# Mixer input stage: a fourth z unit ahead of the first group, ScalarE instead of VectorE reads the turned step sizes, sums over tokens placed ahead of the taps

## What is computed

```python
def mamba2_mixer(u, w_in, conv_w, conv_b, dt_bias, a_log, ...):
    z, xbc, dt_raw = split(u @ w_in, [2048, 2048 + 4096])
    conv = conv_b + sum(xbc_full[:, k:k + t_len] * conv_w[k] for k in range(4))
    xs, bm, cm = split(silu(conv), ...)            # per head, per group
    dt = softplus(dt_raw + dt_bias)
    a = -exp(a_log)
    y, h_last = ssd_scan(xs, dt, a, bm, cm, ssm0)  # chunks of 128 tokens
    ...
def ssd_scan(...):
    cum = cumsum(dtc * a)                          # over the tokens of a chunk
    decay = exp(where(causal, cum_t[l] - cum_t[s], -inf))
    y_intra = einsum(cb * decay, xdt)
    to_end = exp(cum_last - cum)
    ...
```

## Time and profile before

| | |
|---|---|
| median of 3 runs | 1200.87 us (1199.36 to 1201.12) |
| the profiled execution | 1198.53 us |
| its span, first to last instruction | 1196.7 us |
| TensorE (PE) busy | 1186.5 us, 99% |
| VectorE (DVE) busy | 873.0 us, 73% |
| ScalarE (ACT) busy | 696.4 us, 58% |
| GpSimd (POOL) busy | 247.1 us, 21% |

### The profile page before, as it was taken

How to read it: one execution, slowest core, us unless ns; L and a number is a source line. 1 busy time by engine, 2 the same in 40 slices (tenths; PEclk the granted TensorE clock), 3 DMA queues, 4 the chain that set the end, 5 groups by cost and what they waited for, 6 DMA issues and landing times.

```text
span 1196.7 us, 26588 instructions
## 1 busy us (share of the span) xinstructions
PE 1186.5 (99%) x9797; PEld 1157.8 (97%) x9797; DVE 873.0 (73%) x1398; ACT 696.4 (58%) x1132; POOL 247.1 (21%) x351
## 2 busy tenths in 40 slices
PE   9999999999999999999999999999999999999998
PEld 9999999998989899999999999999998899999998
DVE  7667646999999868666745988787468767667448
ACT  6454435777686657555546765555368764544345
POOL 1000002423222202122344333232026310000001
PEclk9999999999999999999999999999999999999999
DMA  8765554755445375866886677656742256555552
GB/s 290 255 202 185 176 178 142 256 181 182 158 160 179 117 219 185 327 216 248 279 299 230 211 269 284 220 172 235 245 163 74 90 167 211 177 181 185 176 178 87
DMA packets 62144, 239.08 MB, mean 200 GB/s; under 512 B 7288, under 2 KB 8480, under 8 KB 57696
## 3 DMA queue, kind: packets, MB, share of 16 engines
q1 hardware_dynamic: 55728, 197.01, 49.0%
q0 software_dynamic: 6064, 40.66, 9.3%
q10 hardware_dynamic: 288, 0.54, 0.1%
HBM read 226.87 MB, written 13.39 MB: 201 GB/s over the span
## 4 chain that ended last, share of the span: by engine, by line
PE 91%; DVE 5%; ACT 2%; issue 1%; DMA 0%; POOL 0%; SPq 0%; DVEq 0%; ACTq 0%
PE bank L479 28%; PE bank L480 28%; PE bank L481 28%; DVE wlo L1520 1%; DVE xact L1788 1%; PE bank L843 1%; DVE xl L1539 1%; PE bank L838 1%; PE bank L652 1%; PE bank L865 1%; PE bank L638 0%; PE bank L895 0%; DMA raw<-weights 0%; ACT whi L1050 0%; PE bank L622 0%
## 5 line engine op out<-in xcount | busy, mean ns | idle before, releaser
L1520 DVE TENSOR_TENSOR wlo<-raw,whi 128x1024 fp32r<-128x1024 f32 x367 | 456.6, 1247 | 237.6 <-ACT whi L1050 236.3
L479 PE MATMUL bank<-xh,whi 128*128 128x264 f32 x2008 | 576.0, 287 | 2.5 <-DVE under L1567 1.5
L480 PE MATMUL bank<-xl,whi 128*128 128x264 f32 x2008 | 569.2, 283 | 0.0
L481 PE MATMUL bank<-xh,wlo 128*128 128x264 f32 x2008 | 568.8, 283 | 0.0
L1050 ACT ACTIVATE whi<-raw 128x1024 fp32r<-128x1024 f32 x367 | 385.4, 1054 | 243.7 <-PE bank L481 231.7
L479 PEld LDWEIGHTS bank<-xh,whi 128*128 128x128 f32 x2008 | 378.2, 188 | 5.9 <-DVE wlo L1520 2.3
L480 PEld LDWEIGHTS bank<-xl,whi 128*128 128x128 f32 x2008 | 378.4, 188 | 0.9
L481 PEld LDWEIGHTS bank<-xh,wlo 128*128 128x128 f32 x2008 | 376.6, 188 | 0.0
L479 PE MATMUL bank<-hh,whi 128*128 (+1 forms) x896 | 255.5, 285 | 0.3 <-ACT gu L1403 0.3
L481 PE MATMUL bank<-hh,wlo 128*128 (+1 forms) x896 | 255.1, 285 | 0.0
L480 PE MATMUL bank<-hl,whi 128*128 (+1 forms) x896 | 254.4, 284 | 0.0
(11 more groups left out here) (331 smaller groups left out, 1024.2 us busy)
## 6 DMA issues: line engine op xcount, KB each, us to landing
raw<-weights SPq DMA_DIRECT2D x367, 512.0 KB, 3.5
under<-ssm POOLq DMA_DIRECT2D x8, 1024.0 KB, 7.3
xact<-ssm POOLq DMA_DIRECT2D x8, 1024.0 KB, 7.8
out_ssm_s<-xact POOLq DMA_DIRECT2D x8, 1024.0 KB, 5.6
xact<-dtx_rows POOLq DMA_DIRECT2D x5, 1024.0 KB, 11.0
zs<-dtx_rows POOLq DMA_DIRECT2D x2, 1024.0 KB, 14.2
x<-xT SPq DMA_DIRECT2D x4, 264.0 KB, 5.6
xact<-stat_rows POOLq DMA_DIRECT2D x2, 528.0 KB, 6.5
```

The source lines that it names most:

```text
L479: pe.matmul(out, whi[:, w, c], rh, start=start, stop=False)
L480: pe.matmul(out, whi[:, w, c], rl, start=False, stop=False)
L481: return pe.matmul(out, wlo[:, w, c], rh, start=False, stop=stop)
L1520: dve.tensor_tensor(wlo[:, s, :], raw[:, s, :], whi[:, s, :].bitcast(F32), ALU.subtract).then_inc(lo_ready, 1)
```

## The change

The order of units becomes dt, z, z, z, z, conv x4 (units 5 to 8), z (9), conv x4 (10 to 13), z (14); from unit 9 on it is as it was. `PRE_AT` becomes 8. TensorE turns in slot 8 and sums in slot 10 as before. ScalarE, in slot 9, copies `dtT` and `da4` out of bank 4 and signals TensorE with a new semaphore `pre_t`; VectorE keeps only `dgl`, now in slot 9. The series for the step sizes is cut 3, 3, 1 over slots 2 to 4 instead of 4, 3 over slots 2 and 3. ScalarE's `cum4` comes in slot 11, ahead of its tap, and `select(0)` with the exponentials in slot 13. VectorE's `pre_sums` comes in slot 11 and `pre_diff` in slot 12, both ahead of the taps of the slot, and `pre_decode` stays in slot 13. ScalarE's doubled high half (units 5 and 6 rounded in a row) is in slot 5 instead of 4 (there units 4 and 5), and the gathers with it. The counts of `pre_d` are one lower. The weights are packed by `SIN`, so the loads follow.

```diff
-Z_FIRST = [0, 1, 2]
-Z_AFTER = {0: [3, 4], 1: [5], 2: [6], 3: [7], 4: [8], 5: [9], 6: [10], 7: [11, 12, 13, 14, 15]}
+Z_FIRST = [0, 1, 2, 3]
+Z_AFTER = {0: [4], 1: [5], 2: [6], 3: [7], 4: [8], 5: [9], 6: [10], 7: [11, 12, 13, 14, 15]}
-PRE_AT = 7
+PRE_AT = 8
# TensorE
-                pe.wait_ge(pre_d, 1)
+                pe.wait_ge(pre_t, 1)
                 for c in range(2):
...
                 mm.then_inc(pre_p, 1)
-                pe.wait_ge(pre_d, 2)
+                pe.wait_ge(pre_d, 1)
                 pe.matmul(bank[7][:, 0:256], ones[32:64, :], dgl[32:64], start=True, stop=True)
...
-                if s_ == PRE_AT + 3:
+                if s_ == PRE_AT + 2:
                     pre_sums()
# ScalarE
-                if 1 < s_ < len(SIN) and s_ != 5:
+                if 1 < s_ < len(SIN) and s_ != 6:
                     ahead("sin", 0, s_)
-                if s_ == 4:
-                    ahead("sin", 0, 5)
+                if s_ == 5:
+                    ahead("sin", 0, 6)
                     gather_sizes()
+                if s_ == PRE_AT + 3:
+                    act.wait_ge(pre_p, 2)
+                    act.activation(cum4, bank[2][:, 0:256], ACT.Copy).then_inc(pre_a, 1)
+                if s_ == PRE_AT + 1:
+                    act.wait_ge(pre_p, 1)
+                    for c in range(2):
+                        act.activation(dtT[c], bank[4][:, 64 * c + 32:64 * c + 64], ACT.Copy)
+                        ins = act.activation(da4[c].rearrange("p (k h) -> p k h", k=4), bank[4][:, 64 * c:64 * c + 32].unsqueeze(1).to_broadcast([P, 4, HEADS]), ACT.Copy)
+                    ins.then_inc(pre_t, 1)
                 if kind == "conv":
                     tap_last(s_, i)
...
-                if s_ == 4:
+                if s_ == 5:
                     gather_steps()
...
-                if s_ == PRE_AT + 3:
-                    act.wait_ge(pre_p, 2)
-                    act.activation(cum4, bank[2][:, 0:256], ACT.Copy).then_inc(pre_a, 1)
                 if s_ == PRE_AT + 5:
-                    act.wait_ge(pre_d, 4)
+                    act.wait_ge(pre_d, 3)
# VectorE
             def pre_tokens():
-                dve.wait_ge(pre_p, 1)
-                for c in range(2):
-                    dve.tensor_copy(dtT[c], bank[4][:, 64 * c + 32:64 * c + 64])
-                    ins = dve.tensor_copy(da4[c].rearrange("p (k h) -> p k h", k=4), bank[4][:, 64 * c:64 * c + 32].unsqueeze(1).to_broadcast([P, 4, HEADS]))
-                ins.then_inc(pre_d, 1)
+                dve.wait_ge(dt_a_step, 5)
...
+                if s_ == PRE_AT + 3:
+                    pre_sums()
+                if s_ == PRE_AT + 4:
+                    pre_diff(0)
+                    pre_diff(1)
                 if last == "conv":
                     conv_taps(li)
...
                 if s_ == 2:
-                    dt_series((15, 13, 11, 9))
+                    dt_series((15, 13, 11))
                 if s_ == 3:
-                    dt_series((7, 5, 3))
+                    dt_series((9, 7, 5))
+                if s_ == 4:
+                    dt_series((3,))
                     dt_end()
                 if s_ == PRE_AT + 1:
                     pre_tokens()
-                if s_ == PRE_AT + 3:
-                    pre_sums()
-                if s_ == PRE_AT + 4:
-                    pre_diff(0)
-                    pre_diff(1)
-                if s_ == PRE_AT + 6:
+                if s_ == PRE_AT + 5:
                     pre_decode()
```

More of the change, by code:

```diff
@@ L268, in trunk_kernel @@
         pre_d = sem("pre_d")
+        pre_t = sem("pre_t")
         pre_a = sem("pre_a")
@@ L1251, in select @@
                 if k == 1:
-                    act.wait_ge(pre_d, 5)
+                    act.wait_ge(pre_d, 4)
                 if k >= 2:
```

## The result

The changed kernel takes 1203.55 us, the median of nine runs (1201.56 to 1205.10), and the kernel before 1199.36 beside it, also of nine (1198.13 to 1201.12). The ratio is 1.0033, 95% interval 1.0025 to 1.0042: about 4.0 us slower. The profiled execution after took 1203.79 us with a span of 1202.0; the one before had 1198.53 and 1196.7. The forecast was 1203.5, on a base of 1200.87 that has turned out 1.5 us too high: direction and place were right, the amount (2.6) was not the whole of it.

What follows compares the result with a forecast made beforehand. TensorE, busy 1186.5 of 1196.7 us, was taken to bound the kernel. The terms -1.44 + 1.63 + 2.27 + 0.17 gave +2.6 us, on 1200.87 a forecast of 1203.5, range 1200.9 to 1205.2.

Steps and rivals of the forecast that it cites:

- What bounds the kernel: Whole kernel: TensorE, busy 1186.5 of 1196.7 us; a change wins or loses only where TensorE stands waiting.
- The hole at unit 9: TensorE's wait for VectorE's take of unit 7: that take comes earlier, 1.44 us gained, 0.2 of the hole left.
- The last sums: Ahead of unit 11: TensorE waits for VectorE's diagonal products, now in slot 9; the 1.44 is spent and 0.19 more, +1.63.
- The copies on ScalarE: Turned step sizes in slot 9: ScalarE needs 0.5 to 1.4 us, taken as 0.7; either bound costs nothing.
- The selection: Head of the first chunk: sums queued behind the take of unit 11 delay ScalarE's first selection; unit 15 2.45 late, term +2.27.
- The first decay: Behind the selection: table load, exponentials, then VectorE's decay product; VectorE 2.63 late at the low half of slot 13, term +0.17.
- The sum: All terms together: -1.44 + 1.63 + 2.27 + 0.17 = +2.6 us.
- rival (c): Behind a larger TensorE hole the granted clock falls to 1.2 GHz; 2.9 us per unit of 24 matmuls, 1206.4; chance 0.03.
- The base: Time of the kernel before that the forecast was added to: 1200.87 us, the median of the runs shown.

Runs made afterwards that it cites:

- e1_dgl8: The changed kernel with VectorE's diagonal products in slot 8 instead of slot 9; 1200.21 us against 1198.49 for the kernel before.
- e6_copies: The kernel before with only the four copies of the turned step sizes moved to ScalarE; 1198.33 us against 1198.58, ratio 0.9998.
- e4_fill: The changed kernel with 11 useless matmuls ahead of the last sums and 16 ahead of the selection; 1201.39 us against 1198.49 for the kernel before.
- e7_late: The kernel before with only sums, differences and selection one slot later, sums and differences ahead of the taps; 1200.90 us against 1198.58.
- e10_after: The changed kernel run and profiled once more without an edit; 1203.99 us against 1198.66 for the kernel before, ratio 1.0043.
- e2_sums10: The changed kernel with sums, differences and first selection one slot earlier, sums and differences behind the taps; 1201.13 us against 1198.49 for the kernel before.

## Why the prediction was right, and where it was short

- **What bounds the kernel.** Right. In the two profiles 4.89 of the 5.3 us in span arise between the common matmul and unit 17; 0.25 lie ahead of it, in the first microseconds of the program, and 0.2 behind unit 17.
- **The hole at unit 9, -1.44.** Measured -1.44, with 0.24 us left of it (forecast 0.2). The take of unit 7, read from starts of rows, held to the hundredth.
- **The last sums, +1.63.** Measured +1.52 (from -1.44 to +0.08). TensorE stood 1.34 us at L928 for VectorE's diagonal products. e1_dgl8 shows the cause: one slot earlier, and 1.29 us come back.
- **The copies on ScalarE, nothing.** Right: four in 0.6 us, between the bounds of 0.5 and 1.4, and off the path. e6_copies alone is worth nothing.
- **The selection, +2.27.** Measured +2.27 (from +0.08 to +2.35) in e4_fill, where the clock plays no part, and +2.25 (from +0.03 to +2.28) in e7_late. The chain behind it held too: on the clock of the kernel before, e4_fill's selection starts at 252.95, against 252.96 in the prediction. The reading was that VectorE would be idle for 2.6 us ahead of the sums; counted on the clock of the changed profile it is 3.92, of which 1.5 belong to a unit 11 that ran at half clock.
- **The first decay, +0.17.** e4_fill has +0.23 (from +2.35 to +2.58), with a hole of 0.4 us left at the decay product. ScalarE's table load took 1.28 us again and the decay began 3.12 us after the selection, 3.13 before. By the figure of the Trainium skill's "ScalarE: Activation LUTs" (Step-by-step: what each stage is for), about 2.7 us with the drain, the sum would have been an estimated 4.0, and the median did move by that; but the row says 1.28 with nothing idle behind it, so the missing 1.4 stood elsewhere. A right total from a wrong term would have been easy to believe here.
- **The sum.** The bare schedule costs 2.58 us by e4_fill's profile and 2.9 by its ratio (1.7 to 4.0), against 2.6 forecast.
- **The step that fell short** is rival (c). The prediction named it, asked for 0.03 of the chance with the words "the trace so far bears it out nowhere within the stage", and left it out of the sum. It took the full clock behind one hole of 1.48 us as evidence for the next holes. The runs show that the clock behind such a hole differs between executions: behind the hole of 1.3 us at L928 it fell in one of three profiles (the changed kernel yes; e10_after and e2_sums10 no), behind the hole of 1.9 to 2.0 us at the selection in four of four (the changed kernel, e10_after, e1_dgl8, e7_late), and with both filled in none. Four of four is no rate: the profiled executions of e1_dgl8 and e7_late, with a mean clock of 0.996, are the slowest and the second slowest of eleven each, and the other twenty have 0.998 to 1.000. Its price was right in kind and too high in amount: 15 or 16 matmuls at 1.2 GHz, 1.5 us, instead of a whole unit of 24, 2.9. The Trainium skill's "TensorE: Matmul & The Clock Gate" (Part 1, What's actually happening) calls the number of slow matmuls at the start of a kernel run-variable, as the chip does not time the transition from the kernel's start. The traces agree that it varies, here in the middle of a kernel: 2 falls and 1 in the stage in two executions of one kernel (+4.89 and +3.38 at unit 17).
- **What is left.** The ratio says +4.0 us (3.0 to 5.0). With no fall, one and two the profiles give +2.6, +3.4 and +4.9, and the nine runs lie 2.2 to 5.7 us above 1199.36, nearly in the order of their mean granted clock: 1201.56 at 0.999, 1203.55 and its neighbours at 0.997, 1205.10 at 0.995. That the middle runs have one or two falls in this stage is argued from this and not shown: only two executions were profiled, a late fall as in e10_after can be among them, and the mean clock also takes in the last microseconds of the program (0.62 from 1195 us on in the kernel before).

The base was a smaller slip. The forecast stood on 1200.87, the median of three runs, while 21 to 33 runs of the same kernel in the other comparisons have medians of 1198.49 to 1198.66. On 1199.36 the forecast of 2.6 gives 1202.0, which is 1.6 below the measured time. That 1203.5 met 1203.55 is luck: this error and the missing falls cancel.

## What to carry to other kernels

Work moved off a saturated engine reaches the bottleneck only at the points where the two meet: list these points (here units 9, 11, 14 and the selection), write the slack of each, and expect the gain at the first to be spent at the one with the least. An instruction that others wait for must not be queued behind a take of the bottleneck's next result: put it where its engine would otherwise be idle. And price a new hole of TensorE of 1 to 2 us above its own length, here up to 1.5 us more for a fall of the clock, in some executions only, so that neither a clean profile nor one with a fall speaks for the median.

## What the runs showed of the hardware that was not expected

TensorE's granted clock fell from 2.4 to 1.2 GHz within the mixer's dense stage, not during a hole but 0.7 to 1.4 us after work had begun again behind one (239.18 is the restart of unit 11 and 239.53 the first slow matmul, 0.98 behind the end of the wait at 238.55; 253.67 and 254.38; 255.18 and 256.6), stayed there for 15 or 16 matmuls 0.22 us apart, and came back by itself. In this stage it happened behind holes of 1.3 to 2.0 us, not behind those of 0.2 to 0.5, and in the same kernel in one execution and not in the next. With idle-filling matmuls it stayed at 2.4 GHz (1.00 in the profile of e4_fill, 0.999 or 1.000 in nine of its ten runs). But a hole is not needed: the fall at 954.1 us in e10_after had none longer than 0.3 us in the 39 us ahead of it, and came behind 64 matmuls of 4 columns. What decides in a given execution, why the late fall came only in some, and why the hole of 1.5 us at unit 9 was never followed by a fall in the profiles of the kernel before, e6_copies and e7_late, stays open.
